# First mixing stage: projections in another order, the inverse between them, attention and units in one loop

## The chip, the cores and the metric

The kernel runs on one core of a Trainium2 chip. The metric is the device time of one execution in microseconds (us); a time is the median of several runs. The engines named here are TensorE (PE in the profile, PEld is its weight load), VectorE (DVE), ScalarE (ACT), GpSimd (POOL) and SyncE (SP), which only issues loads. Each runs its own queue in order, and they meet by semaphores.

## The reference, cut to what matters

Two blocks of two layers each, 512 tokens, width 1024, all in float32. The change lies in the mixer of the second block's first layer. Its input `p = h @ ab_w_in` is split into the columns of differential attention (q, k, v) and those of an RWKV-7 time mix (14 blocks of 128 columns: r, k, v, a low-rank decay and rate input, and a gate input):

```python
p = h @ ab_w_in[j]
qa, ka, va = split_cols(p[..., :A_COLS], A_SIZES)
oa = diff_attention(qa, ka, va, ...)      # 4 heads, softmax(q0 k0) - lam * softmax(q1 k1), times v, rmsnorm
ob = rwkv7_time_mix(p[..., A_COLS:], ...) # 8 heads of 64, state 64x64 per head
mix = jnp.concatenate([oa, ob], axis=-1) @ ab_w_out[j]
x = x + mix
```

Attention, per head and block of 128 queries: two masked softmaxes over up to 512 keys, mixed, times the values. The time mix shifts its input by one token (`mu`), makes from the low-rank input a decay (`w0`, `w2`) and a rate (`a0`, `a2`), normalises the key per head (`kk`), and runs per head `S = S * w + (S @ a) b^T + v k^T`, with `y = S @ r`; then a group norm, a bonus term of `r * rk * k`, and a gate.

## The kernel before, in words

Activations lie transposed: channels on the 128 partitions, the 512 tokens along the free axis. Every f32 product with a weight is three `fp32r` matmuls (high by high, high by low, low by high). A weight chunk (128 x 1024) is loaded by SyncE into one of two raw buffers; ScalarE makes its high part (`weights_hi`, L433), VectorE the low part (`weights_lo`, L445), into a ring of four. Both run three chunks ahead and stand in the queues among the other work: step n makes chunk n + 2. A projection is 24 matmuls of 512 columns. PSUM has eight banks; `K.take` makes TensorE wait until the bank's last user has been read.

The stage (`ab_tensor`, `ab_vector`, `ab_scalar`, `ab_gpsimd`; the order is written out by hand, one list for each engine) runs so:

1. Fourteen rwkv projections in the order `MIXED`: keys (4 to 7), then 12 (decay and rate input) and 13 (gate input), then r and v blocks in turn. VectorE drains each (`ab_project_vector`, times 1/rms), ScalarE scales its own copy, and VectorE adds the shifted one (`mixed_in`). Between them stand the small steps of the time mix for each of four pairs of heads a: `ab_low_tensor` (two low-rank matmuls), `ab_rates_scalar` (two sigmoids and a scaling of the rate for the key), `ab_sums_vector` (a scan of decays), `ab_decays_scalar` (exps), `ab_kk_vector`, `ab_bonus_tensor`, `ab_decayed_vector`, and `ab_lower_tensor`/`ab_lower_vector` (the strictly lower 32 x 32 blocks L, always in banks 6 and 7). Three work tiles (`E.sets`) exist twice, and a uses set a % 2.
2. Four q and four k projections with rope; GpSimd turns rows by DMA (`turn_gpsimd`). The rest of step 1's small steps lies here. When all of L is there, GpSimd takes it through DRAM so that each partition holds one 32 x 32 block (M). Then `linear_tok`: the values, 96 matmuls.
3. `ab_inverse_vector`, the inverse of the triangular blocks on VectorE: part 0 (two 16 x 16 diagonal blocks, rows 14 down to 0), parts 1 to 8 (the off-diagonal block). Parts 0 and 1 stand before attention, parts 2 to 8 between its steps, half a part a step.
4. Attention, 16 steps (head hd, query block t), as a pipeline over 20: scores in banks 0 to 3 (two pairs in turn), mask and maximum on VectorE (L2164, L2167), exp on ScalarE (L2379), mix on VectorE, a transposing matmul with a diagonal (`pt`), values (`pv`).
5. The inverse goes back through DRAM to L. Then 16 units i of the time mix (pair of heads a, 128 tokens t) as a pipeline over 18: `rwkv_b` (four transposes; the ml products in banks 1 and 2, masked by VectorE), `rwkv_c`, `rwkv_d`, `rwkv_e` (G, R and N in banks 4, 6 and 5). The row norm of attention (`rs`, spreads, `y2a`) lies in its first steps.
6. The chain of 15 states (`E.state(n)`), each from the last by a matmul and a VectorE add. Then the output projections and the next layer.

The pieces are tied by order: what a list puts behind a waiting instruction waits as well.

Of the kernel before, what the change touches and what calls it, by code (L numbers as in the profile page):

```python
# [16 lines left out]
P = 128  # L17
# [143 lines left out]
class Kernel:  # L161


    def __init__(self, nc, io, ctx):
# [14 lines left out]
        if self.base > before:  # L179
# [18 lines left out]
                    for i in range(NH)]  # L198
        at += 2 * NH * SLOT
# [1475 lines left out]
NC = 16  # L1675

# [40 lines left out]
class Ab:  # L1717
# [3 lines left out]
    def __init__(self, K):  # L1721
# [29 lines left out]
        sets = [self.vt[:, i, :] for i in range(4)] + [spare[:, 0:T], spare[:, T:2 * T]]  # L1751
        self.sets = [sets[0:3], sets[3:6]]
        self.M = spare[:, 0:1024].rearrange("p (s t) -> p s t", s=32)
        self.blocks = spare.rearrange("p (b z) -> p b z", b=2)[:, :, 0:512].rearrange("p b (j t) -> p b j t", t=32)
        self.tm = raw[:, 0:1024]

        H = K.hmem
        self.sqa = H[:, 0:2048].rearrange("p (k n) -> p k n", k=4)
        self.ya = H[:, 2048:4096].rearrange("p (k n) -> p k n", k=4)
        self.pr = [H[:, 4096 + T * i:4096 + T * i + T] for i in range(6)]  # L1760
        self.pt = [H[:, 7168 + T * i:7168 + T * i + T] for i in range(2)]
        self.dg = [K.nb[0][:, P * i:P * i + P] for i in range(3)]
# [8 lines left out]
                            vt[:, 640 * i:640 * i + 640], nb[:, T * i:T * i + T]) for i in range(3)]  # L1771
# [29 lines left out]
    def scores(self, K, i):  # L1801

        return K.ps[:, 2 * (i % 2):2 * (i % 2) + 2, :]
# [47 lines left out]
def ab_bonus_tensor(K, w, a):  # L1851
    acc = K.take(w, ("bonus", a), K.V)
    w.wait_ge(*K.V["rk", a])
    mm(w.e, v4(acc), K.cc("bones"), K.ab.be(a), True, True).then_inc(*K.P.up(("bonus", a)))
# [14 lines left out]
def ab_attention_tensor(K, w):  # L1869
    E, e = K.ab, w.e  # L1870
    w.wait_ge(*K.V["k", "rope", 3])
    for i in range(20):
        if i < 16:
            hd, t = i // 4, i % 4
            both = E.scores(K, i)
            for c in range(2):
                r = slice(64 * c, 64 * c + 64)
                K.take(w, ("score", i, c), K.A, bank=2 * (i % 2) + c)
                done = mm(e, both[:, c, 0:(t + 1) * P], E.q[r, hd, t * P:(t + 1) * P], E.k[r, hd, 0:(t + 1) * P],
                          True, True)  # L1880
# [1672 lines left out]
```

## Time and profile before

| | |
|---|---|
| median of 3 runs | 2768.85 us (2764.5 to 2778.71) |
| the profiled execution | 2759.99 us |
| its span in the profile | 2758.2 us |
| TensorE busy | 2653.2 us (96%) |
| VectorE busy | 1453.7 us (53%) |
| ScalarE busy | 985.1 us (36%) |
| mean granted TensorE clock | 0.977 |

Times in the profile count from the start of the span. Busy is the time in which an engine works on at least one instruction. The granted clock is the share of full TensorE speed (2.4 GHz) that the chip allowed; 0.50 is 1.2 GHz. An f32 matmul shows as two instructions. In brackets behind an instruction stands how long its engine was idle before it and who ended that. The changed stage lies between 881.8 and 1240.6 us.

### The profile page before, as it was taken

What the parts mean: (1) busy time and instruction counts of PE and PEld (TensorE: products, weight loads), DVE (VectorE), ACT (ScalarE), POOL (GpSimd) and SP (SyncE); (2) the same over time, 40 slices, a digit from 0 to 9 for tenths busy, and PEclk for the clock granted to TensorE, in tenths of its full rate; (3) what the DMA queues carried; (4) which work ended last, traced back from release to release, by engine and by line L of the source; (5) the groups of instructions that cost most, each with busy time, mean ns of one, the idle gap of its engine ahead of it and who ended that gap; (6) DMA issues with size and microseconds to landing.
All of it is one profiled execution on the core that took longest, in us unless ns stands there. A gap on an engine that the chain in (4) does not pass through costs nothing.

```text
span 2758.2 us, 32180 instructions
## 1 busy us (share of the span) xinstructions
PE 2653.2 (96%) x13236; PEld 2112.1 (77%) x13236; DVE 1453.7 (53%) x1905; ACT 985.1 (36%) x1660; POOL 528.3 (19%) x554
## 2 busy tenths in 40 slices
PE   8989998999999998899999999999999998999998
PEld 7777877788888665686788888888878745888886
DVE  8875995643434688546433334343354466533432
ACT  3235545422323533543322223222233445322221
POOL 5711001322200020101222102221002124222200
PEclk9999999999999998899999999999999989999999
DMA  4433112222232231002232332323323300222332
GB/s 154 100 96 113 62 46 69 84 100 93 96 102 93 71 99 32 28 2 69 100 100 92 95 104 92 99 98 93 102 78 122 116 16 1 78 98 99 97 93 86
DMA packets 76932, 232.19 MB, mean 84 GB/s; under 512 B 14961, under 2 KB 16241, under 8 KB 76529
## 3 DMA queue, kind: packets, MB, share of 16 engines
q1 hardware_dynamic: 64176, 212.46, 23.8%
q0 software_dynamic: 4400, 9.71, 1.6%
q10 hardware_dynamic: 8208, 7.96, 0.9%
q8 instruction: 104, 1.70, 0.3%
q14 instruction: 44, 0.35, 0.0%
HBM read 220.13 MB, written 5.77 MB: 82 GB/s over the span
## 4 chain that ended last, share of the span: by engine, by line
PE 78%; DVE 10%; ACT 5%; POOL 4%; issue 1%; DMA 0%; ACTq 0%; DVEq 0%; POOLq 0%
PE ps L358 78%; POOL mem L375 3%; DVE mem L375 3%; DVE part L445 2%; ACT part L433 1%; DVE mem L388 1%; PE ps L369 1%; ACT mem L509 0%; POOL mem L3269 0%; DVE mem L393 0%; DVE mem L3032 0%; DVE mem L408 0%; DVE mem L553 0%; DVE mem L634 0%; DVE mem L2167 0%
## 5 line engine op out<-in xcount | busy, mean ns | idle before, releaser
L358 PE MATMUL ps<-part,part 128*128 128x512 f32 (+1 forms) x9870 | 2249.8, 389 | 33.0 <-DVE part L445 8.5
L358 PEld LDWEIGHTS ps<-part,part 128*128 128x128 f32 x9870 | 1838.7, 189 | 439.6 <-issue 15.8
L445 DVE TENSOR_TENSOR part<-mem,part 128x1024 fp32r<-128x1024 f32 (+2 forms) x419 | 563.2, 1351 | 597.6 <-ACT part L433 597.3
L433 ACT ACTIVATE part<-mem 128x1024 fp32r<-128x1024 f32 (+2 forms) x419 | 415.6, 1003 | 241.9 <-DMA mem<-in_ffa_down 55.9
L375 DVE TENSOR_TENSOR mem<-ps,mem 128x512 f32<-128x512 f32 (+1 forms) x266 | 176.7, 664 | 297.1 <-PE ps L358 288.1
L358 PE MATMUL ps<-mem 128*64 128x64 f32 (+13 forms) x2568 | 264.5, 310 | 35.8 <-ACT mem L2385 10.3
L358 PEld LDWEIGHTS ps<-mem 128*64 128x64 f32 (+5 forms) x2568 | 180.7, 165 | 109.5 <-issue 41.5
L517 POOL TENSOR_TENSOR mem<-mem 128x512 f32<-128x512 f32 x62 | 80.6, 1300 | 713.2 <-ACT mem L509 712.2
L1669 POOL TENSOR_TENSOR mem<-mem 128x512 f32<-128x512 f32 x88 | 113.8, 1293 | 381.5 <-ACT mem L1657 381.5
L1671 POOL TENSOR_TENSOR part<-mem,part 128x512 fp32r<-128x512 f32 x88 | 113.8, 1293 | 353.0 <-ACT part L1660 353.0
L1660 ACT ACTIVATE part<-mem 128x512 fp32r<-128x512 f32 x88 | 55.6, 632 | 327.9 <-DVE mem L375 327.9
L1657 ACT ACTIVATE mem<-mem 128x512 f32<-128x512 f32 x88 | 55.6, 632 | 313.3 <-DVE mem L375 313.2
L522 ACT ACTIVATE part<-mem,prm 128x512 fp32r<-128x512 f32 x56 | 40.4, 722 | 241.1 <-DVE mem L636 169.6
L375 DVE TENSOR_TENSOR mem<-mem 128x512 f32<-128x512 f32 (+15 forms) x205 | 109.6, 534 | 26.5 <-PE ps L358 8.4
L375 POOL TENSOR_TENSOR mem<-mem 128x32 f32<-128x32 f32 (+5 forms) x83 | 85.2, 1026 | 178.6 <-ACT mem L1545 172.0
L636 DVE SCALAR_TENSOR_TENSOR mem<-ps,mem 128x512 f32<-128x512 f32 x32 | 22.1, 692 | 172.6 <-PE ps L358 172.6
L1405 DVE SCALAR_TENSOR_TENSOR mem<-mem,prm 128x512 f32<-128x512 f32 x142 | 97.1, 750 | 0.2
L358 PE MATMUL ps<-mem,cst 128*128 128x512 f32 (+9 forms) x162 | 81.8, 607 | 8.5 <-DVE mem L375 4.1
L3269 POOL TENSOR_TENSOR mem<-mem 128x512 f32<-128x512 f32 (+3 forms) x64 | 45.8, 736 | 123.8 <-DVE mem L375 123.7
L509 ACT ACTIVATE mem<-mem 128x512 f32<-128x512 f32 x64 | 39.6, 618 | 66.7 <-DVE mem L636 66.7
L358 PE MATMUL ps<-cst,mem 128*64 128x64 f32 (+2 forms) x360 | 53.9, 291 | 9.0 <-ACT mem L1145 8.2
L1704 POOL DMA_DIRECT2D mem<-mem x56 | 27.5, 498 | 169.9 <-PE ps L358 107.1
(191 smaller groups left out, 1182.8 us busy)
## 6 DMA issues: line engine op xcount, KB each, us to landing
mem<-in_ffa_gate SPq DMA_DIRECT2D x44, 512.0 KB, 3.3
mem<-in_ffa_up SPq DMA_DIRECT2D x44, 512.0 KB, 3.3
mem<-in_ffb_gate SPq DMA_DIRECT2D x44, 512.0 KB, 3.2
mem<-in_ffb_up SPq DMA_DIRECT2D x44, 512.0 KB, 3.3
mem<-in_ffa_down SPq DMA_DIRECT2D x32, 512.0 KB, 3.5
mem<-in_ffb_down SPq DMA_DIRECT2D x32, 512.0 KB, 3.5
mem<-in_w_odd SPq DMA_DIRECT2D x24, 512.0 KB, 3.3
mem<-in_w_ab SPq DMA_DIRECT2D x22, 512.0 KB, 3.2
```

What stands on the lines that cost most here:

```text
L358: return e.matmul(out, l, r, start=start, stop=stop, skip_group_check=True)
L375: w.e.tensor_tensor(out, a, b, op).then_inc(*w.own.up(*names))
L433: w.e.activation(K.wts[c % NH].h[:, 0:n], K.raws[c % NR][:, 0:n], ACT.Copy).then_inc(*K_A.up(("w", c)))
L445: w.e.tensor_tensor(t.l, K.raws[c % NR][:, 0:n], t.hf, SUB).then_inc(*K.V.up(("w", c)))
L517: w.e.tensor_tensor(ss, ss, sq[k % 2], ADD).then_inc(*K.G.up(("ss", s, k)))
L522: w.e.activation(K.h[k].h, K.x[:, k, :], ACT.Copy, scale=gain(k)).then_inc(*K.A.up(("h", s, k)))
L1405: e.scalar_tensor_tensor(out=c, in0=g[:, k:k + T], scalar=K.pc("conv_w", 31 * o + k), in1=c, op0=MUL, op1=ADD).then_inc(*K.V.up(("tap", o, ...
L1657: w.e.activation(t, t, ACT.Silu).then_inc(*K.A.up(("silu", s, o)))
L1660: w.e.activation(K.hidden.hid[o].h, t, ACT.Copy).then_inc(*K.A.up(("hid", s, o)))
L1669: w.e.tensor_tensor(t, t, K.rstd, MUL).then_inc(*K.G.up(("factor", s, o)))
L1671: w.e.tensor_tensor(K.hidden.hid[o].l, t, K.hidden.hid[o].hf, SUB).then_inc(*K.G.up(("hid", s, o)))
L3269: w.e.tensor_tensor(pr, pr, E.st[u % 4][:, 4 + g:5 + g].to_broadcast([P, n]), MUL).then_inc(*K.G.up(("npr", u, g)))
```

## The change: what it does

- `MIXED` becomes `[12, 4, 5, 6, 7, 0, 8, 1, 9, 2, 10, 3, 11, 13]`: the decay and rate input is projected first, then the keys; the gate input last. The four low-rank pairs follow projections 2 and 3, the sigmoids of all four a stand in ScalarE's steps 3 and 4, the decays in its steps 5 and 6, the head sums of the key norm behind projection 6 (before 5).
- `E.sets` has four sets, taken from the space of q, k and v; `wait`s keep the owners apart. The bonus product goes to `sets[a][2]` and not to `be(a)`.
- L(0) to L(3) follow projections 11, 12, 13 and q(0). L is taken through DRAM after the turn of q(1), M read after that of q(2). The diagonal blocks of the inverse (`ab_diagonal_vector`) stand in six pieces between the q and k projections, parts 1 to 6 before the loop, parts 7 and 8 in its first step.
- Attention and units are one loop of 22 steps; the unit u = j - 4. Scores use banks 1 and 2 only, the pair that the ml products of the units also use; `pt` has bank 6, the head outputs bank 7, G moves into the second half of R's bank 4. Probabilities and `wide` move into three slots of the weight ring.
- The norm of attention's rows comes at the loop's end; two spreads in its last step, two in the chain of states, with `spread` and `y2a` of VectorE between its states.

```diff
-MIXED = [4, 5, 6, 7, 12, 13, 0, 8, 1, 9, 2, 10, 3, 11]
+MIXED = [12, 4, 5, 6, 7, 0, 8, 1, 9, 2, 10, 3, 11, 13]
...
 def ab_tensor(K, w):
...
-        if n == 5:
+        if n == 2 or n == 3:
+            ab_low_tensor(K, w, 2 * n - 4)
+            ab_low_tensor(K, w, 2 * n - 3)
+        if n == 6:
             ab_heads_tensor(K, w, "kk", E.be, lambda a: K.A["kk2", a])
...
+        if n == 8 or n == 9:
+            ab_spread_tensor(K, w, "kk", 2 * n - 16, E.factors)
+            ab_spread_tensor(K, w, "kk", 2 * n - 15, E.factors)
+        if n > 10:
+            ab_lower_tensor(K, w, n - 11)
...
+            if n == 0:
+                ab_lower_tensor(K, w, 3)
+            if 0 < n < 5:
+                ab_bonus_tensor(K, w, n - 1)
...
+def ab_units_tensor(K, w):
+
     w.wait_ge(*K.V["k", "rope", 3])
+    for j in range(STEPS_AB):
+        u = j - DELAY
+        if j < 16:
+            ab_score_tensor(K, w, j)
+        if 0 <= u - 1 < 16:
+            rwkv_c_tensor(K, w, u - 1)
+        if 0 <= u - 2 < 16:
+            rwkv_e_tensor(K, w, u - 2)
+        if 0 <= j - 2 < 16:
+            ab_turned_probs_tensor(K, w, j - 2)
+        if 0 <= u < 16:
+            rwkv_b_tensor(K, w, u)
+        if 0 <= u - 1 < 16:
+            rwkv_d_tensor(K, w, u - 1)
+        if 0 <= j - 3 < 16:
+            ab_values_tensor(K, w, j - 3)
...
 def ab_vector(K, w):
...
-        if n == 6:
+        if n == 4 or n == 5:
+            ab_sums_vector(K, w, 2 * n - 8)
+            ab_sums_vector(K, w, 2 * n - 7)
+        if n == 7:
             rstd_vector(K, w, ("ms", "kk"), E.factors[0:8, :], K.acc("ms", "kk")[0:8, :], 1.0, 1e-12)
...
+        if n == 8:
+            for a in range(4):
+                ab_keys_vector(K, w, a)
+        if 9 <= n < 13:
             ab_kk_vector(K, w, n - 9)
+        if n > 11:
+            ab_lower_vector(K, w, n - 12)
...
+    diagonal = ((14, 9), (8, 6), (5, 5), (4, 3), (2, 2), (1, 1))
...
+        if o > 2:
+            ab_diagonal_vector(K, w, *diagonal[o - 3])
...
+def ab_units_vector(K, w):
+
+    E = K.ab
+    for j in range(STEPS_AB):
+        u = j - DELAY
+        if j < 16:
+            ab_max_vector(K, w, j)
+        if 0 <= j - 1 < 16:
+            ab_mix_vector(K, w, j - 1)
+        if j == 0:
+            ab_inverse_vector(K, w, 7)
+            ab_inverse_vector(K, w, 8)
+        if 0 <= u - 2 < 16:
+            rwkv_e_vector(K, w, u - 2)
...
+        if 0 <= u < 16:
+            rwkv_ml_vector(K, w, u)
+        if 0 <= u + 1 < 16:
+            rwkv_b_vector(K, w, u + 1)
...
 def ab_scalar(K, w):
...
+        if n == 2:
+            w.wait_ge(*K.V["mixed_in", 0])
+            e.activation(E.wa[0:64, :], E.wa[0:64, :], ACT.Tanh).then_inc(*K.A.up("wa"))
+        if 3 <= n < 7:
+            a = n - 3
+            w.wait_ge(*K.V["mixed_in", 1 + a])
             e.activation(E.al(a), E.ka(a), ACT.Copy, scale=K.pc("kk", a)).then_inc(*K.A.up())
             w.wait_ge(*K.A.now)
             e.activation(E.be(a), E.al(a), ACT.Square).then_inc(*K.A.up(("kk2", a)))
-        if n == 4:
+        if n == 3 or n == 4:
+            ab_rates_scalar(K, w, 2 * n - 6)
+            ab_rates_scalar(K, w, 2 * n - 5)
+        if n == 5:
             w.wait_ge(*K.V["lam"])
             e.activation(E.lam[:, 2:4], E.lam[:, 0:2], ACT.Exp).then_inc(*K.A.up("lam"))
+        if n == 5 or n == 6:
+            ab_decays_scalar(K, w, 2 * n - 10)
+            ab_decays_scalar(K, w, 2 * n - 9)
+        if n == 7:
+            for a in range(4):
+                ab_keys_scalar(K, w, a)
             rstd_scalar(K, w, ("ms", "kk"), E.factors[0:8, :])
```

## Rows read from the trace of the kernel before

**Rows 1.** The page: chain that ended last, shares by engine.
```profile
PE 78%; DVE 10%; ACT 5%; POOL 4%; issue 1%; DMA 0%; ACTq 0%; DVEq 0%; POOLq 0%
```
**Rows 2.** Windows: stretch, its us; PE, PEld, DVE, ACT, POOL busy; granted clock; DMA.
```profile
881.80:976.90 95.10, 89.03 (x350) 62.71 (x349) 61.73 (x78) 47.76 (x65) 0.00 (x0) 0.98 0.23 76
976.90:1058.80 81.90, 77.59 (x356) 61.43 (x356) 66.38 (x108) 24.05 (x34) 19.46 (x37) 0.94 0.34 97
1058.80:1120.60 61.80, 44.53 (x232) 29.54 (x232) 49.58 (x96) 35.20 (x109) 3.71 (x5) 0.83 0.06 18
1120.60:1222.25 101.65, 93.91 (x1163) 77.61 (x1163) 52.06 (x93) 55.90 (x153) 10.55 (x16) 0.92 0.03 9
1222.25:1240.57 18.32, 16.36 (x465) 14.70 (x465) 6.61 (x16) 0.37 (x1) 0.00 (x0) 1.00 0.01 3
```
**Rows 3.** Timeline of TensorE: start, us, line, shape, count [idle before].
```profile
881.82 27.49 PE L358 MATMUL ps<-part,part 128*128 128x512 f32 x120
...
965.48 1.13 PE L358 MATMUL ps<-mem 64*128 64x512 f32 x4
...
994.56 2.08 PE L358 MATMUL ps<-mem 64*128 64x128 f32 x16 [3.52 <-DVE mem L375]
...
1017.06 1.16 PE L358 MATMUL ps<-mem 64*128 64x128 f32 x16
...
1036.84 22.06 PE L358 MATMUL ps<-part,part 128*128 128x512 f32 x96 [0.75 <-ACT mem L1687]
```
**Rows 4.** Timeline of ScalarE: a copy, a table load, a sigmoid, decays, weight copy.
```profile
894.98 0.72 ACT L2443 ACTIVATE mem<-mem 128x512 f32<-128x512 f32 x1 [2.09 <-DVE mem L375]
...
933.37 1.28 ACT L2400 ACT_TABLE_LOAD   x1
934.66 0.69 ACT L2400 ACTIVATE mem<-ps,prm 128x512 f32<-128x512 f32 x1
...
948.57 0.63 ACT L2414 ACTIVATE mem<-mem 128x512 f32<-128x512 f32 x1
...
950.55 1.04 ACT L433 ACTIVATE part<-mem 128x1024 fp32r<-128x1024 f32 x1
```
**Rows 5.** Timeline of VectorE: low part, mix, products, L, inverse part 0, ml mask.
```profile
951.63 1.23 DVE L445 TENSOR_TENSOR part<-mem,part 128x1024 fp32r<-128x1024 f32 x1
...
953.68 0.75 DVE L388 SCALAR_TENSOR_TENSOR mem<-mem,prm 128x512 f32<-128x512 f32 x1
...
960.20 3.60 DVE L375 TENSOR_TENSOR mem<-mem 128x512 f32<-128x512 f32 x5
...
992.72 1.78 DVE L375 TENSOR_TENSOR mem<-ps,cst 32x256 f32<-32x256 f32 x4
...
1044.54 0.09 DVE L403 MEMSET mem<- 128x32 f32 x1 [1.57 <-DMA mem<-scratch]
...
1056.81 0.62 DVE L408 TENSOR_REDUCE mem<-mem 128x30 f32<-128x450 f32 x1
...
1170.79 0.96 DVE L375 TENSOR_TENSOR mem<-ps,cst 128x768 f32<-128x768 f32 x1 [1.00 <-PE ps L358]
```
**Rows 6.** Windows of five us, columns as rows 2: two with low clock.
```profile
995.00:1000.00 5.00, 5.00 (x22) 3.45 (x21) 3.73 (x6) 1.07 (x2) 0.00 (x0) 0.50 0.34 104
...
1135.00:1140.00 5.00, 5.00 (x18) 2.77 (x18) 0.96 (x1) 2.12 (x6) 0.00 (x0) 0.50 0.00 0
```
**Rows 7.** Window of ten units, columns as rows 2.
```profile
1164.20:1215.10 50.90, 50.90 (x722) 44.77 (x721) 25.52 (x51) 31.62 (x91) 5.56 (x9) 1.00 0.01 2
```
**Rows 8.** Groups of VectorE from 1061.5 to 1120.6: busy, mean ns, idle before.
```profile
L2167 DVE TENSOR_REDUCE mem<-ps 128x2 f32<-128x256 f32 (+3 forms) x16 | 13.2, 825 | 0.6
...
L375 DVE TENSOR_TENSOR mem<-mem 128x768 f32<-128x768 f32 (+3 forms) x7 | 8.2, 1170 | 0.2
L2164 DVE TENSOR_TENSOR ps<-ps,cst 128x256 f32<-128x256 f32 x15 | 6.4, 426 | 2.9 <-PE ps L358 2.8
L408 DVE TENSOR_REDUCE mem<-mem 128x64 f32<-128x768 f32 (+3 forms) x7 | 5.3, 763 | 0.2
```

More of the change, by code:

```diff
@@ L198, in __init__ @@
                     for i in range(NH)]
+        self.slots = [mem[:, at + 2 * i * SLOT:at + 2 * (i + 1) * SLOT] for i in range(NH)]
         at += 2 * NH * SLOT
@@ new lines, in ab_score_tensor, with ab_turned_probs_tensor @@
+def ab_score_tensor(K, w, i):
+    E = K.ab
+    hd, t = i // 4, i % 4
+    both = E.scores(K)
+    for c in range(2):
+        r = slice(64 * c, 64 * c + 64)
+        K.take(w, ("score", i, c), K.A, bank=1 + c)
+        done = mm(w.e, both[:, c, 0:(t + 1) * P], E.q[r, hd, t * P:(t + 1) * P], E.k[r, hd, 0:(t + 1) * P], True, True)
+    done.then_inc(*K.P.up(("score", i)))
+def ab_turned_probs_tensor(K, w, u):
+    E = K.ab
+    acc = K.take(w, ("pt", u), K.A, bank=6)
+    w.wait_ge(*K.V["mixed_pr", u])
+    w.wait_ge(*K.A["diag", u])
+    for kt in range(u % 4 + 1):
+        done = mm(w.e, acc[:, kt * P:(kt + 1) * P], E.pr[2 * u % 6][:, kt * P:(kt + 1) * P], E.dg[u % 3], True, True)
+    done.then_inc(*K.P.up(("pt", u)))
@@ L2120, in ab_lower_vector, with ab_diagonal_vector, ab_inverse_vector @@
     K.V.also(("L", a), ("L", a, 0), ("L", a, 1))
-def ab_inverse_vector(K, w, part, steps=(0, 1)):
+def ab_diagonal_vector(K, w, first, last):
+    E = K.ab
+    B, tm = E.blocks, E.tm
+    if first == 14:
+        w.wait_ge(*K.counts["shuffle"]["M"])
+        memset(w, E.M.rearrange("p s t -> p (s t)")[:, 0:1024:33], 1.0)
+    for s in range(first, last - 1, -1):
+        n = 15 - s
+        tmv = tm[:, 0:2 * n * n].rearrange("p (b t j) -> p b t j", b=2, t=n)
+        tt(w, tmv, B[:, :, s + 1:16, s + 1:16].rearrange("p b j t -> p b t j"),
+           b(B[:, :, s, s + 1:16], [P, 2, n, n], 2), MUL)
+        reduce(w, B[:, :, s, s + 1:16], tmv, ADD)
+def ab_inverse_vector(K, w, part):
     E = K.ab
@@ new lines, in ab_inverse_vector, with ab_max_vector @@
+        tt(w, tmv, b(B[:, 0, s0:s0 + 4, s0:16], [P, 4, 16, n], 2),
+           b(M12[:, s0:16, :].rearrange("p j t -> p t j"), [P, 4, 16, n], 1), MUL)
+        reduce(w, M12[:, s0:s0 + 4, :], tmv, ADD, *(["inverse"] if part == 8 else []))
+def ab_max_vector(K, w, i):
+    E = K.ab
+    t = i % 4
+    n = (t + 1) * P
+    both, st = E.scores(K), E.st[i % 4]
+    w.wait_ge(*K.P["score", i])
+    w.e.tensor_tensor(both[:, :, t * P:n], both[:, :, t * P:n], b(K.cc("negmask"), [P, 2, P], 1), ADD).then_inc(
+        *K.V.up())
+    w.wait_ge(*K.V.now)
+    w.e.tensor_reduce(st[:, 0:2], both[:, :, 0:n], AX, MAX, negate=True).then_inc(*K.V.up(("max", i)))
@@ L2394, in ab_rates_scalar @@
 def ab_rates_scalar(K, w, a):
     E = K.ab
-    if a > 1:
-        w.wait_ge(*K.V["decayed", a - 2])
     w.wait_ge(*K.P["decay", a])
-    w.e.activation(E.sets[a % 2][0], K.acc("decay", a), ACT.Sigmoid, bias=K.pc("w0", a)).then_inc(
+    w.e.activation(E.sets[a][0], K.acc("decay", a), ACT.Sigmoid, bias=K.pc("w0", a)).then_inc(
         *K.A.up(("decay", a)))
```

505 lines of the change are left out of this document (225 added, 280 removed).

## The prediction

> **What bounds the kernel now.** I read the chain that ended last first: TensorE holds 78% of it and VectorE 10% [rows 1], so a step counts only where it makes TensorE wait or lets it stop waiting. The change lies in one stage, so I next read that stage in five stretches [rows 2]: the rwkv projections 1 to 13 (95.1 us), q, k and av (81.9), attention (61.8), the units (101.65) and the chain of states (18.3). The reader is to see where TensorE is idle: 6.1 us of the first, 4.3 of the second, 17.3 of the third and 7.7 of the fourth. In the third VectorE is busy 49.6 of 61.8: it bounds attention, because the inverse sits between its steps. In the middle of the fourth TensorE has no gap at all and a unit costs 50.9/10 = 5.09 us [rows 7]. So 17 + 8 us of gaps can be won by laying attention over the units. To win them the change starts its VectorE work earlier and reorders the first two stretches; I then ran each engine's queue through them, with the durations of rows 3 to 5, from 881.8 us, where TensorE starts projection 1.
>
> **Stretch 1, projections 1 to 13 (before 95.1).** TensorE's work: 13 projections at 27.49/5 = 5.50 [rows 3] are 71.5; four pairs of low-rank matmuls at 1.13, 4.5; four head sums and four spreads, each one matmul of 512 columns, priced at 1.0 by that same row, 8.0; three L blocks at 1.1, 3.2. Sum 87.2. To it come these waits:
> - After projection 2 (ends 892.8) the low-rank pair needs tanh. ScalarE ends the projection's own copy at 895.7 [rows 4], loads a table (1.28), takes the tanh (0.6, as the sigmoid): 897.6. Wait 4.8.
> - After projection 3 the second rate matmul needs the bank of decay(0), and the next ones those of the following sigmoids. They come behind, on ScalarE: VectorE's drain 0.7, own copy, key copy and square 0.65 each, table load 1.28, four sigmoids at 0.6: 6.5 us after the projection's end. TensorE has 1.4 of work for it. Wait 5.1. Projection 4 starts at 912.0.
> - After projection 6 (ends 928.4) the last head sum needs the square of key 3. From the end of projection 5 (922.9, rates done at about 922.5) run: weight copy 1.0, its low part 1.25, drain 0.7, own copy, key copy and square 1.95, table load 1.5 with the small exp, two sets of decays at 1.98 (948.57 to 950.55 [rows 4]) 4.0, weight copy 1.0, low part 1.25, drain 0.7, and the last three ScalarE steps 1.95: 938.1. TensorE has three head sums (about 2.9) meanwhile. Wait 6.8. It is the queue that counts: projection 6's drain on VectorE stands behind a low part whose high part stands behind the decays.
> - After projection 8, four key scalings (2.9) on ScalarE and the reciprocal on VectorE: wait 1.0.
> - L(1) takes the banks of L(0), which VectorE empties at the end of its step 12: drain 0.7, mix 0.75, four operations of kk(3) at 0.72 [rows 5], L(0) 1.78, with gaps 6.3. L(2) likewise: 0.7 + 0.75 + 1.78 and gaps, 3.4.
> Waits 27.4, against 6.1 before. 87.2 + 27.4 = 114.6: **+19.5**.
>
> **The clock.** After the wait of 3.52 us at 994.56 [rows 3] the granted clock was 0.50 over the next 5 us [rows 6], the lower of the two levels; that and the rest of the recovery cost about 3 us. Four of the new waits are longer than that one; 4 x 3 = 12 at most on the path, and some of it is absorbed by the wait behind it. I take **+9**; ends 0 and 20.
>
> A table switch is in three of these waits. The row shows a load of 1.28 us and the sigmoid starting at 934.66, right behind it [rows 4]. The Trainium skill (ScalarE: Activation LUTs, What ACT_TABLE_LOAD costs) gives about 1.38 us of drain beside each load. By it the three waits would be longer by 4.1 us together and the forecast 2783; the rows show no drain, so the measurement decides.
>
> **Stretch 2, q, k, av (before 83.9 to VectorE's first score at 1060.8).** VectorE's queue from the start of q(0): eleven low parts 13.0, eight ropes at 2.1, 16.8, L(2) and L(3) 3.6, bonus products and outputs 5.8, decayed products (8) 5.8, mix, cos and sin 3.6, the diagonal blocks of the inverse 12.9 (1044.54 to 1057.43 [rows 5]), its part 1 3.3 and parts 2 to 6 10.8 (seven pieces 8.2 + 5.3 [rows 8] less parts 7 and 8, 2.8). Sum 75.6. Waits for turned rows and the first transfer of M about 5, and it starts 1 us early: 79.7, **-4.2**. TensorE's own work there is 44 + 1.1 + 3.7 + 22.1 [rows 3] = 71: the moved inverse is not hidden to its end; TensorE stands about 8 us before the loop, on VectorE.
>
> **Stretch 3, the loop (before 161.4 from 1060.8 to the first state).** Work of TensorE: 16 units at 5.09 are 81.4; attention 44.5 busy at a granted 0.83 [rows 2], some 39 at full clock with its four norm sums; two row spreads 2.1: 122. A step has 5.09 + 35/16 = 7.3 of TensorE. VectorE has 4.8 us a step (25.5/10 of units [rows 7] and (49.6 - 13.5)/16 of attention) and ScalarE 5.4 (31.6/10 and 35.2/16), so both fit. Gaps: scores have one pair of banks now, so in steps 0 to 3 score (0.8), mask and maximum (19.6/16 [rows 8]) and exps (1.1) follow one another, 3.4 a step and 1.2 for parts 7 and 8: 15 in all, of which TensorE works 5: +10. Steps 4 and 5 +2.6, steps 6 to 15 0.3 each (the ml masks, 0.96 [rows 5], before the next score, with only 0.7 to 1.5 of TensorE work between), tail 1.5. Sum 139. The clock: 1135 to 1140 was busy throughout and still at 0.50 [rows 6]; the loop starts after an 8 us wait and five light steps, +8. 147: **-14.4**; ends 130 and 165.
>
> **Stretch 4, the states (before 18.3).** Two spreads on TensorE (+1.1); the eight VectorE pieces of 0.7 fit into the idle of 18.3/15 - 6.6/15 = 0.78 of each state [rows 2]: **+1.1**, at worst +4.
>
> **Sum.** 19.5 + 9 - 4.2 - 14.4 + 1.1 = +11.0 us. The profiled execution, 2759.99, would become 2771; it is 8.9 below the median of the three runs, 2768.85, so the predicted median is 2780. A measurement of this kernel can tell some 0.5% (13.8 us) from no change: 2755 to 2783 is the same.
>
> **Rivals.** (a) The loop packs as meant: 8 us of fill on 122 give 130, and the clock in stretch 1 costs 2 because TensorE still issues small matmuls in the waits. 19.5 + 2 - 4.2 - 31.4 + 1.1 = -13, near 2755, and with 3 us less waiting there 2752: faster. For it: TensorE had no gap in ten units. Against it: the waits of stretch 1 follow from queue order. (b) Slower: the single pair of banks. Score, maximum, exp (3.4 together, as above), ml matmuls (0.9, estimated), ml mask, next score is a ring through three engines; on average 5.3 us, and with the longest tiles, whose maximum and exps take half as long again, about 7, near TensorE's own 7.3. It decides from a step of 7.6 on; at 8.8 it adds 1.2 x 16 = 19: 2799. (c) The clock stays at its lower level behind each wait longer than in the one row: 20 in place of 9, and 2791: slower. (d) The change does not do what it says: ScalarE or VectorE in the loop hold the units back to where they were, 161 for the loop: 2794, slower; it shares its chance with (b).
>
> **Chances.** Forecast 0.44, (a) 0.16, (b) with (d) 0.26, (c) 0.14. Faster 0.16, same 0.44, slower 0.40. The likeliest case alone reaches from 2764 to 2790; the range 2752 to 2802 leaves out the outer part of (a) and of (b).
>
> **What would show it.** The first q projection starts some 28 us later than the 976.9 of before, with TensorE waits of 4 to 7 us after projections 2, 3, 6 and 12 ended by ScalarE or VectorE; the granted clock is lower behind them; TensorE waits about 8 us before the first score; then a step of the loop takes 7.3 to 7.9 us with TensorE busy nearly throughout; and the first state comes near 1232. It is wrong if the waits in the projections are under 15 us together, if the loop takes under 135 or over 160, or if the states take over 23.

## The result, and the profile after

| | before | after |
|---|---|---|
| median | 2768.73 us (8 runs, 2764.43 to 2778.71) | 2788.82 us (8 runs, 2780.72 to 2795.85) |
| ratio | | 1.0067, 95% interval 1.0052 to 1.0082 |
| profiled execution | 2759.99 us | 2787.78 us |
| the stage, first rwkv projection after its entry to the first output matmul | 881.82 to 1240.57, 358.75 us | 892.77 to 1266.71, 373.94 us |
| mean granted TensorE clock | 0.977 | 0.970 |

The change makes the kernel slower by 0.67%, 18.6 us by the ratio. The stage in the profile is 15.2 us longer; it is entered 10.95 us later and what lies behind it takes 1.7 us more. Those two parts run unchanged code. How far they move by themselves is an experiment below; so from here on the stage alone is compared.

The chain that ended last, on the page after: TensorE and VectorE hold a little more of it [rows 1].

```profile
PE 80%; DVE 11%; ACT 5%; issue 1%; POOL 1%; DMA 0%; ACTq 0%; DVEq 0%; POOLq 0%
```

The windows of the kernel after that answer to the stretches of before [rows 2, 7]: projections to q(0), then q, k and values, then the wait and the loop, four steps and more of the loop alone, and the states. Columns as there.

```profile
892.77:1019.15 126.38, 100.09 (x394) 71.56 (x393) 71.26 (x94) 50.82 (x73) 0.00 (x0) 0.88 0.18 57
1019.15:1091.50 72.35, 71.60 (x310) 57.14 (x309) 59.02 (x94) 16.18 (x20) 19.52 (x37) 0.97 0.38 110
1091.50:1242.05 150.55, 129.54 (x1395) 103.11 (x1393) 94.02 (x181) 88.20 (x262) 13.62 (x21) 0.91 0.05 15
1141.70:1215.20 73.50, 70.59 (x853) 59.56 (x852) 43.71 (x94) 47.41 (x150) 6.57 (x11) 1.00 0.01 2
1242.05:1266.71 24.66, 23.10 (x470) 20.84 (x469) 12.38 (x24) 2.52 (x4) 0.00 (x0) 0.73 0.01 2
```

The reader is to see 26.3 us of TensorE idle in the first (6.1 before), and a clock of 0.88 where it was 0.98; almost no gap in the second; a loop whose middle runs at full clock; and a chain of states at 0.73 where it ran at 1.00.

The waits of the first stretch, in the timeline of TensorE after (start, duration, line, shape, count, idle before and its releaser):

```profile
908.73 3.78 PE L359 MATMUL ps<-mem 64*128 64x512 f32 x8 [4.79 <-ACT mem L2592]
...
923.82 3.23 PE L359 MATMUL ps<-mem 64*128 64x512 f32 x6 [3.76 <-ACT mem L2540]
926.97 17.00 PE L359 MATMUL ps<-part,part 128*128 128x512 f32 x72
...
953.74 1.88 PE L359 MATMUL ps<-mem,cst 128*8 128x512 f32 x2 [7.09 <-ACT mem L2598]
...
1004.46 2.08 PE L359 MATMUL ps<-mem 64*128 64x128 f32 x16 [6.38 <-DVE mem L376]
1006.47 7.28 PE L359 MATMUL ps<-part,part 128*128 128x512 f32 x24
...
1017.14 2.08 PE L359 MATMUL ps<-mem 64*128 64x128 f32 x16 [3.39 <-DVE mem L376]
```

They are tanh (4.79), the rate's bank (3.76, after 1.1 of work), the square of key 3 (7.09), the banks of L(0) (6.38) and of L(1) (3.39); 0.88 lies between. The clock shows in the durations: a projection of 24 matmuls takes 7.28 right behind a wait, and 17.00/3 = 5.67 once it has recovered; two L blocks' 16 matmuls take 2.08 in place of 1.16.

The entry of the loop, same view:

```profile
1092.62 0.49 PE L359 MATMUL ps<-mem 64*128 64x128 f32 x4
1103.79 1.57 PE L359 MATMUL ps<-mem 64*128 64x256 f32 x4 [10.67 <-ACT mem L2440]
1107.82 2.82 PE L359 MATMUL ps<-mem 64*128 64x384 f32 x6 [2.47 <-ACT mem L2440]
1112.14 4.21 PE L359 MATMUL ps<-mem 64*128 64x512 f32 x10 [1.50 <-ACT mem L2440]
```

TensorE has issued the first score and stands 10.67 us for VectorE's first maximum and the exps behind it; each further score waits for the ring of mask, maximum and exp.

The chain of states, same view, and two windows inside it:

```profile
1240.08 2.03 PE L359 MATMUL ps<-mem,cst 4*128 4x512 f32 x4 [1.00 <-ACT mem L559]
1242.05 6.92 PE L359 MATMUL ps<-mem 64*64 64x64 f32 x128
1248.90 1.12 PE L359 MATMUL ps<-mem,cst 4*128 4x512 f32 x2
1249.95 1.12 PE L359 MATMUL ps<-mem 64*64 64x64 f32 x32
1251.00 1.12 PE L359 MATMUL ps<-mem,cst 4*128 4x512 f32 x2
1252.05 9.16 PE L359 MATMUL ps<-mem 64*64 64x64 f32 x192
...
1266.71 3.02 PE L359 MATMUL ps<-part,part 128*128 128x512 f32 x12 [0.90 <-DVE mem L376]
```

```profile
1243.00:1248.00 5.00, 5.00 (x100) 5.00 (x98) 2.77 (x5) 1.26 (x2) 0.00 (x0) 0.50 0.00 0
...
1252.00:1257.00 5.00, 5.00 (x95) 4.95 (x96) 2.75 (x5) 1.26 (x2) 0.00 (x0) 0.51 0.02 3
```

TensorE is busy in every one of these ten microseconds and yet at the lower level of 1.2 GHz. In windows of one microsecond the clock is at 0.50 from 1242 to 1248.7 and again from 1252 to 1258.5, 13 of the 24.7 us. A state is 16 matmuls, 32 records; the 128 at 1242.05 are four states in 6.92, 1.73 each, against the 18.3/15 = 1.22 of before.

### The profile page after: what moved, and what is told of

It reads as the page before. It is cut to its first block, busy times and chain, and to the rows that moved or that the text cites. A ratio compares the mean times of both kernels' runs of the same rounds, so it can differ in the third digit from the quotient of the medians.

```text
span 2786.0 us, 32135 instructions
## 1 busy us (share of the span) xinstructions
PE 2663.1 (96%) x13236; PEld 2126.6 (76%) x13236; DVE 1461.0 (52%) x1905; ACT 978.7 (35%) x1659; POOL 524.6 (19%) x554
## 4 chain that ended last, share of the span: by engine, by line
PE 80%; DVE 11%; ACT 5%; issue 1%; POOL 1%; DMA 0%; ACTq 0%; DVEq 0%; POOLq 0%
PE ps L359 80%; DVE mem L376 4%; DVE part L446 2%; ACT part L434 1%; PE ps L370 1%; DVE part L376 1%; ACT mem L510 0%; DVE mem L409 0%; DVE mem L3145 0%; POOL mem L3382 0%; DVE mem L389 0%; DVE mem L394 0%; DVE mem L554 0%; DVE mem L635 0%; ACT mem L3335 0%
## 5 line engine op out<-in xcount | busy, mean ns | idle before, releaser
L359 PE MATMUL ps<-mem 128*64 128x64 f32 (+11 forms) x2568 | 261.9, 312 | 47.6 <-ACT mem L2440 16.1
L376 DVE TENSOR_TENSOR mem<-mem 128x512 f32<-128x512 f32 (+14 forms) x205 | 113.8, 555 | 19.4 <-ACT mem L1187 7.8
```

Source lines behind the costliest of these rows:

```text
L359: return e.matmul(out, l, r, start=start, stop=stop, skip_group_check=True)
L376: w.e.tensor_tensor(out, a, b, op).then_inc(*w.own.up(*names))
```

## The experiments

All are written against the kernel after; where a section says that a kernel builds on spread_low or one_load, its edit is shown against that one. Where a median stands, it comes with the ratio to the kernel before on the same chip. The stage is the stretch defined above, in the profiled execution of each. For every kernel that was timed, the stage less the 358.75 us of before agrees within 5 us with what its ratio says of 2770 us.

| | stage us | median us | ratio (95%) |
|---|---|---|---|
| after | 373.9 | 2788.82 | 1.0067 (1.0052 to 1.0082) |
| split | 408.7 | 2819.18 | 1.0164 (1.0138 to 1.0191) |
| early_l | 359.5 | 2775.63 | 1.0006 (0.9989 to 1.0023) |
| late_decays | 367.4 | 2782.17 | 1.0026 (1.0009 to 1.0043) |
| spread_low | 346.9 | 2761.68 | 0.9950 (0.9930 to 0.9971) |
| pool_low | 349.4 | 2766.38 | 0.9969 (0.9953 to 0.9986) |
| delay5 | 350.4 | 2768.39 | 0.9981 (0.9957 to 1.0006) |
| late_inverse | 355.9 | 2767.93 | 0.9979 (0.9963 to 0.9996) |
| norm_split | 343.8 | 2757.70 | 0.9958 (0.9938 to 0.9977) |
| before_again | 358.2 | one run, 2770.23 | |
| one_load | 346.9 | one run, 2759.68 | |
| norm_late | 349.3 | one run, 2764.68 | |
| rows_after | 376.5 | one run, 2790.16 | |

### before_again: how far unchanged code moves

The kernel before, once more, no edit.

> The kernel before, profiled once more, to see how far the part ahead of the stage, which the change does not touch, moves from one execution to the next. If the 10.95 us by which the changed kernel's profile entered the stage later (892.77 against 881.82) is variation between executions, this profile enters between 882 and 893, with a total that is higher by about as much, and the stage itself again takes 358 to 360 us. If the changed kernel's code costs something ahead of the stage, it enters at 882 to 883 again.

Measured: it enters at 882.01, which by itself decides nothing, and the stage takes 358.2. But this execution took 10.2 us longer than the first, and all of it lies behind the stage (span 2768.4 against 2758.2, first output matmul at 1240.19 against 1240.57). The kernels of this study, all with the same code ahead of the stage, entered it between 880.73 (norm_split) and 893.61 (early_l). So some 10 us of either unchanged part is variation between executions, and neither the 10.95 ahead of the stage nor a single total says anything of the change. The guess that a fixed cost sits ahead of it fell with norm_split and late_inverse (881.12).

### split: what laying attention over the units is worth

```diff
-DELAY = 4
+DELAY = 19
...
-        if j > 20:
-            for hd in (2 * j - 42, 2 * j - 41):
+        if j == 21:
+            for hd in (0, 1):
...
-        if j >= 7 and j % 4 == 3:
+        if 7 <= j < 20 and j % 4 == 3:
```

(beside the delay, this keeps the number of row spreads and of copies of attention's outputs as it was)

> The changed kernel with a lag of 19 steps in place of 4, so that attention runs alone and the units follow it; everything else stays, the inverse between the projections too. Theory (the loop wins by laying attention over the units): the stretch from VectorE's first score to the first state, 139.7 us in the changed kernel, grows to attention alone at the score ring's 3.9 us a step (62) and units at 5.09 with their start (98), 158 to 162; the time is 18 to 22 us above the changed kernel, near 2809. Rival (the loop's saving came from taking the inverse out of attention, and the overlap gives nothing more, since score, maximum and exp hold the units back): the stretch stays under 146 and the time within 6 us of the changed kernel, 2783 to 2795.

Measured: 2819.18, 27 us above the kernel after by the ratios (0.0097 x 2773). Its stage is 34.7 longer. From VectorE's first score to the first state pass 177.6 us, against 139.7 in the kernel after and an expected 158 to 162: the theory holds, and the size was put too low. The 27 us are what the overlap is worth within this order; against the kernel before, which ran attention and units apart in 161.4 us with two pairs of score banks, the loop gains 21.7. TensorE's timeline of split:

```profile
1128.26 2.33 PE L359 MATMUL ps<-mem 64*128 64x512 f32 x8 [0.91 <-ACT mem L2440]
1134.46 9.64 PE L359 MATMUL ps<-mem 128*128 128x128 f32 x48 [3.88 <-ACT mem L2468]
...
1203.82 2.83 PE L359 MATMUL ps<-mem 128*128 128x64 f32 x52 [0.47 <-DVE mem L376]
```

Alone, the score steps wait 3.9 us a head for the head's copies (L2468), and each unit 0.47 for VectorE; in the merged loop other work fills both. The loop is a gain; the loss is elsewhere.

### early_l: the banks of L

VectorE reads L(0) to L(2) one projection earlier, directly behind the matmuls that made them.

```diff
-        if n > 11:
-            ab_lower_vector(K, w, n - 12)
+        if n > 10:
+            ab_lower_vector(K, w, n - 11)
...
         if o == 0:
-            ab_lower_vector(K, w, 2)
```

> The changed kernel, with only VectorE's reading of the blocks L(0), L(1), L(2) one projection earlier (behind projections 11, 12, 13). Theory (the six waits of TensorE in the projections are the loss, and each is the order of one queue): the waits of 6.38 and 3.39 us behind projections 12 and 13 go, and with them the low clock behind them, 10 to 15 us less than the changed kernel, near 2776. Rival (the waits are hidden in VectorE's lateness at the loop's entry, which is then 10 us more of waiting there): the time stays within 3 us of the changed kernel.

Measured: 2775.63, ratio 1.0006: this edit alone takes back 14.4 us of the stage and brings the changed kernel level with the one before. TensorE's timeline of early_l, at L(2):

```profile
1006.41 1.16 PE L359 MATMUL ps<-mem 64*128 64x128 f32 x16 [0.65 <-DVE mem L376]
```

The wait of 6.38 at L(1) is gone and that of 3.39 at L(2) has become 0.65, 9.1 us in all, and a block's matmuls take 1.16 in place of 2.08: the waits took the clock with them, which is the other 5 us. At TensorE's first score early_l is 14.4 us ahead of the kernel after. Behind it the loop takes 1.7 us more and the states 2.3 less, with the same code in both.

### late_decays: ScalarE's queue ahead of the last square

```diff
-        if n == 5 or n == 6:
-            ab_decays_scalar(K, w, 2 * n - 10)
-            ab_decays_scalar(K, w, 2 * n - 9)
+        if n == 6:
+            ab_decays_scalar(K, w, 0)
+            ab_decays_scalar(K, w, 1)
...
             rstd_scalar(K, w, ("ms", "kk"), E.factors[0:8, :])
+            ab_decays_scalar(K, w, 2)
+            ab_decays_scalar(K, w, 3)
```

> The changed kernel, with only ScalarE's decays (0, 1) behind the square of key 3 in step 6 and decays (2, 3) behind the norm factor in step 7, before in steps 5 and 6 ahead of that square. Theory: TensorE's wait of 7.09 us for the last head sum falls to under 2, with the clock 6 to 9 us less than the changed kernel, near 2781. Rival (TensorE then waits as long for the spreads or for weights, as ScalarE's work is only shifted): within 3 us of the changed kernel, 2786 to 2792.

Measured: 2782.17, stage 6.5 us shorter than after. TensorE's timeline of late_decays, at the last head sum and at L(1):

```profile
949.64 1.02 PE L359 MATMUL ps<-mem,cst 128*8 128x512 f32 x2 [3.31 <-ACT mem L2598]
...
999.08 2.08 PE L359 MATMUL ps<-mem 64*128 64x128 f32 x16 [7.36 <-DVE mem L376]
```

7.09 fell to 3.31, not to the "under 2" of the theory, and 1.0 of it came back at L(1), 6.38 to 7.36. The median came within 1.2 us of the 2781 expected.

### spread_low: the low-rank pairs apart, with both edits above

```diff
-        if n == 2 or n == 3:
-            ab_low_tensor(K, w, 2 * n - 4)
-            ab_low_tensor(K, w, 2 * n - 3)
+        if n == 3 or n == 5:
+            ab_low_tensor(K, w, n - 3)
+            ab_low_tensor(K, w, n - 2)
```

(and the sigmoids in ScalarE's steps 3 and 5, the sums in VectorE's steps 4 and 6)

> The changed kernel with both edits above and the low-rank pairs taken apart: pairs 0, 1 behind projection 3 and pairs 2, 3 behind projection 5, their sigmoids in ScalarE's steps 3 and 5, their sums in VectorE's steps 4 and 6. Theory: all six waits in the projections (27.4 us) fall to under 5 and the granted clock in that stretch rises from 0.88 to 0.97 or more; the stretch goes from 126.4 to 92 to 97 us. Some 25 to 32 us less than the changed kernel, 2757 to 2764, which is below the kernel before by 5 to 12. Rival (VectorE, not TensorE, bounds from projection 9 to the loop, so the waits move to the loop's entry): 10 to 15 less than the changed kernel, with a TensorE wait of over 20 us before the second score.

Measured: 2761.68, ratio 0.995 (0.9930 to 0.9971): faster than both kernels. Its projections take 99.5 us to q(0) where the kernel after takes 126.4. The time came as expected (2757 to 2764), the stretch did not quite: its waits are 8.8 us together and not under 5, its clock is 0.95 and not 0.97, and 92 to 97 us had been put. TensorE's timeline of spread_low at three of the waits left:

```profile
933.95 1.88 PE L359 MATMUL ps<-mem,cst 128*8 128x512 f32 x2 [5.36 <-ACT mem L2597]
...
979.54 1.16 PE L359 MATMUL ps<-mem 64*128 64x128 f32 x16 [1.85 <-DVE mem L376]
...
1070.89 1.57 PE L359 MATMUL ps<-mem 64*128 64x256 f32 x4 [10.72 <-ACT mem L2439]
```

Its stage is 27.0 us shorter than that of the kernel after, with the same loop: the order of small steps in the projections was the loss, and the loop doesn't need it.

### one_load: a wait that only moves

```diff
-        if n == 5:
-            w.wait_ge(*K.V["lam"])
-            e.activation(E.lam[:, 2:4], E.lam[:, 0:2], ACT.Exp).then_inc(*K.A.up("lam"))
...
         if n == 6:
+            w.wait_ge(*K.V["lam"])
+            e.activation(E.lam[:, 2:4], E.lam[:, 0:2], ACT.Exp).then_inc(*K.A.up("lam"))
             ab_decays_scalar(K, w, 0)
```

> spread_low, with ScalarE's small exp of lambda behind the square of key 3 and directly ahead of the decays, which use the same table. Theory (ScalarE's queue sets the 5.36 us wait before the last head sum): one table load (1.28) and the small exp leave the queue ahead of the square, the wait falls to 3.9 to 4.1 us and the q projections start 1.3 us earlier. Rival (VectorE's drain and mix of projection 6 come last there, whatever ScalarE does): the wait stays within 0.4 us of 5.36.

Measured: the wait fell as the theory says, and the rest did not. TensorE's timeline of one_load:

```profile
928.97 1.88 PE L359 MATMUL ps<-mem,cst 128*8 128x512 f32 x2 [3.84 <-ACT mem L2597]
...
975.22 2.08 PE L359 MATMUL ps<-mem 64*128 64x128 f32 x16 [2.89 <-DVE mem L376]
```

5.36 became 3.84, but L(1)'s wait grew by 1.0 (1.85 to 2.89) with a lower clock behind it (2.08 for the block in place of 1.16), and a new one of 0.28 came where the 0.67 at L(2) went; q(0) starts 99.3 us after the entry (99.5 in spread_low), and the stage is 346.9 in both. From projection 8 on it is VectorE's queue, 5.6 us a step and 7.6 with an L block, that sets the pace.

### pool_low: GpSimd in VectorE's place

The low parts of the four value chunks on GpSimd, otherwise spread_low.

```diff
-            out.append((io[name][k:k + 2].rearrange("k p n -> p k n"), 2 * n, False))
+            out.append((io[name][k:k + 2].rearrange("k p n -> p k n"), 2 * n, name == "w_av"))
...
+        if n > 5:
+            weights_lo_gpsimd(K, w, K.first[4] + 17 + n)
...
+    weights_lo_gpsimd(K, w, K.first[4] + 26)
```

> spread_low, with the low parts of the four value chunks made by GpSimd, which stands idle there, and not by VectorE. Theory: TensorE's wait of 10.72 us before the second score is VectorE's queue of the second stretch (inverse, ropes, low parts: 81.3 us against 71.5 of TensorE). Four low parts of 1.22 leave it: the wait falls by 4.5 to 5 us to about 6, and the median by as much, near 2757 where spread_low had 2762. Rival: GpSimd takes longer over them (its 128x256 operation took 0.67 us, so 128x1024 about 2.7, and more if the two engines slow each other), so the values' matmuls wait for their chunks, or VectorE's own operations grow by what was saved: the first score comes less than 2 us earlier and the time is the same or up to 5 us more.

Measured: the rival. The wait before the second score grew from 10.72 to 15.31 and the stage by 2.5 us. The median is 2766.38, 4.7 above spread_low's, but the two intervals of the ratio overlap. VectorE's timeline of pool_low, and then GpSimd's over the same time:

```profile
1033.77 5.07 DVE L376 TENSOR_TENSOR mem<-mem 128x512 f32<-128x512 f32 x4
...
1039.31 5.58 DVE L376 TENSOR_TENSOR mem<-mem 128x288 f32<-128x288 f32 x1
```

```profile
1033.77 2.42 POOL L458 TENSOR_TENSOR part<-mem,part 128x1024 fp32r<-128x1024 f32 x1
...
1039.66 4.75 POOL L458 TENSOR_TENSOR part<-mem,part 128x1024 fp32r<-128x1024 f32 x2
```

The same product of 128x288 on VectorE in spread_low:

```profile
1038.37 0.70 DVE L376 TENSOR_TENSOR mem<-mem 128x288 f32<-128x288 f32 x1
```

0.70 became 5.58: VectorE's operation began just before GpSimd's two of 2.4 us and ended when both were over. Three such places cost 2.3, 4.9 and 2.1 us, 9.3 in all, against 4.9 saved. The Trainium skill (Trainium Architecture — The Big Picture, What this means for kernel authors) calls the port that the two share an exclusive lock and not a split of bandwidth; by that rule, the trace agrees: the 0.35 us ahead of GpSimd's two and the 0.48 behind them are enough for the whole of VectorE's 0.70, so nothing of it need have gone on beside them.

### delay5 and late_inverse: the loop's entry

Both build on spread_low.

```diff
-DELAY = 4
+DELAY = 5
```

(and the two spreads of the loop stay in its step 21, as in split) and for late_inverse also

```diff
-    for part in range(1, 7):
+    for part in range(1, 5):
...
-        if j == 0:
-            ab_inverse_vector(K, w, 7)
-            ab_inverse_vector(K, w, 8)
+        if j < 2:
+            ab_inverse_vector(K, w, 5 + j)
+        if j == 2:
+            ab_inverse_vector(K, w, 7)
+            ab_inverse_vector(K, w, 8)
```

> spread_low, with the units five steps behind attention, not four. It is the control for late_inverse. TensorE has one more light score step before the first unit (about 3.5 us of ring for 2.2 of its work, so +1.3) and one more step of units alone at the end, in which the norm's reciprocals and root lie a step further from the chain of states, so the waits of 1.0 us at the loop's end go. Sum near zero: within 2 us of spread_low's stage (346.9 us). If the fall of the clock at the start of the chain stands on those waits, it goes too and the stage is 2 to 4 us shorter.

> delay5, with parts 5 and 6 of the inverse in the loop's first two steps and parts 7 and 8 in its third. Theory (the wait of 10.7 us at the loop's entry is VectorE's queue): the first score comes 5.6 us earlier, the parts fill VectorE's idle 1.9 and 2.1 of the steps behind, and the inverse is back through DRAM (9.2 us) about when unit 0 wants it. The entry wait falls to about 5, the stage is 2 to 4 us shorter than delay5's. Rival: the score ring of VectorE and ScalarE pays for each part in full, and unit 0 waits for the transfer: the stage stays within 1 us of delay5's, since it is then the inverse's end plus its transfer, not the first score, that starts the units.

Measured: delay5's stage is 3.5 us longer than spread_low's, outside the 2 us expected, late_inverse's 5.5 longer again. In late_inverse the entry wait fell from 11.19 to 7.62, but the three that follow grew (2.79, 2.02, 1.56), a later one of 1.58 became 2.77, and the clock, back at 1.00 for a few us in between, was at 0.50 again from 1083 to 1103, where delay5 stayed at 1.00 from 1088 on. VectorE waits 2.25 for the inverse's transfer before the first unit: the units start when the inverse is back, and earlier scores bought nothing, as the rival said; the size of the loss was foreseen by neither. In delay5 the units alone at the loop's end bring a wait of their own for the ml mask, queued on VectorE behind 3.52 us of reciprocals. TensorE's timeline of delay5:

```profile
1202.74 5.46 PE L359 MATMUL ps<-mem 128*128 128x64 f32 x60 [2.86 <-DVE mem L376]
```

Over ten runs each, the two differ by nothing (0.9981 and 0.9979), so the 5.5 us between their profiles is not shown by their times.

### rows_after, norm_late, norm_split: what lowers the clock in the states

rows_after moves all four spreads of the kernel after behind the chain. norm_late (on spread_low) cuts the norm's reciprocals in four between states 3 to 6 and issues the spreads at states 9, 10, 12 and 13. norm_split (on one_load):

```diff
-        if c == 4 or c == 5:
-            ab_rows_tensor(K, w, c - 2)
+        if c in (4, 5, 8, 9):
+            w.wait_ge(*K.A["rstd", ("ms", "subln")])
+            ab_rows_tensor(K, w, (4, 5, 8, 9).index(c))
...
             recip(w, E.rs[0:4, 0:256], E.rs[0:4, 0:256])
+        if j == 21:
             recip(w, E.rs[0:4, 256:T], E.rs[0:4, 256:T], ("inverse", ("ms", "subln")))
```

(not shown: the loop has no spread any more, the square root stands behind the loop on ScalarE, and VectorE's steps for the spreads stand behind states 6, 7, 10 and 11)

> The changed kernel, with all four row spreads and what VectorE does with them behind the chain of states. Theory: the granted clock falls in the states because of what the spreads bring (two four-matmul spreads with their waits at 1240.08 and 1248.90 to 1252, each followed by 0.50). Then the chain of states runs at 1.00 and takes 18.3 to 19 us, as in the kernel before; behind it TensorE issues 2.1 us of spreads and waits about 3 for VectorE and ScalarE (0.75 + 0.6 + 0.7 for the first row block, 1.45 for each further one against 0.7 of matmuls), and from the first state to the first output matmul pass 23 to 24 us against 24.66. Rival: it is the thinned end of the merged loop, or the small matmuls of the states, that brings the clock down; then the chain shows 0.50 for 5 us or more again, takes 21 to 23, and 26 to 28 us pass.

> spread_low, with the reciprocals of attention's row norm (3.5 us of VectorE in one piece, ahead of the last unit's steps in the queue) cut into four and put between the additions of states 3 to 6, the square root behind the last unit's copies on ScalarE, and the row spreads at states 9, 10, 12 and 13. From the last unit's group of matmuls (the one with the wait of 0.56) to the first output matmul passed 21.1 us in the kernel before, 29.9 in the changed one and 32.4 with all spreads behind the chain, where the clock fell to 0.50 at the chain's start behind a wait of 1.90, with no spread before it. Theory: the first fall of the clock comes from TensorE's waits at the loop's end, which stand behind the reciprocals; then the chain starts at 1.00 behind waits of 0.57 and 0.56, and 25 to 27 us pass (21.1, 2.1 of spreads, up to 3 for a second fall behind the spreads). Rival: the clock falls there whatever the norm does, because the last steps of the loop are light; then the chain's start is at 0.50 again and 28 us or more pass.

> one_load, with the second half of the reciprocals of attention's row norm (1.76 us of 3.5) behind VectorE's last unit step, the square root behind ScalarE's copies of the last unit, and the row spreads at states 4, 5, 8 and 9. In norm_late the chain began at a clock of 1.00 behind waits of 0.56 and 0.58, but its states came 1.50 us apart while the reciprocals lay between them, and a fall of the clock followed in its second half. Theory (waits of TensorE around the loop's end bring the falls): the waits stay at about 0.6, no reciprocal lies between the states, the chain runs at 1.00 but for a few us, and from the last unit's group with the wait of 0.56 to the first output matmul pass 24 to 27 us against 29.9 of spread_low. The stage takes 341 to 344 us against 346.9, and the median comes near 2758 where spread_low had 2762 (ratio 0.993 to 0.994). Rival: the four spreads of 512 columns from four rows, or a period of their own, bring the falls, so two falls of 5 us come again; 28 to 30 us pass and the ratio is 0.995 as for spread_low.

Measured, from the last unit's group with its wait of 0.56 to the first output matmul: before 21.1 us, after 29.9, rows_after 32.4, norm_late 31.9, norm_split 30.6. TensorE's timeline of rows_after, and two windows of it:

```profile
1233.29 19.49 PE L359 MATMUL ps<-mem 64*64 64x64 f32 x464 [1.90 <-ACT mem L2490]
1252.71 5.74 PE L359 MATMUL ps<-mem,cst 4*128 4x512 f32 x8
1261.57 4.53 PE L359 MATMUL ps<-part,part 128*128 128x512 f32 x12 [3.12 <-DVE mem L376]
```

```profile
1237.00:1240.00 3.00, 3.00 (x62) 3.00 (x62) 0.85 (x2) 0.00 (x0) 0.00 (x0) 0.50 0.03 5
...
1246.00:1249.00 3.00, 2.74 (x80) 2.52 (x82) 0.88 (x3) 0.00 (x0) 0.00 (x0) 1.00 0.00 0
```

Here the clock falls at the chain's start with no spread before it, behind a wait of 1.90, and 28.3 us pass from the first state to the first output matmul where 23 to 24 were expected: that first fall does not need the spreads, so the theory does not hold as put. With that wait cut to about 0.6, in norm_late and norm_split, the chain starts at 1.00: the first fall comes with TensorE's waits at the loop's end (from the one of 1.00 on in these runs), where the last unit's copies stand behind the norm's reciprocals and root. But a second fall then came behind the spreads, and a long one: 17 us in norm_late, 14 in norm_split. TensorE's timeline of norm_split and a window:

```profile
1196.81 1.12 PE L359 MATMUL ps<-mem 64*64 64x64 f32 x32 [0.58 <-ACT mem L2489]
1198.44 3.54 PE L359 MATMUL ps<-mem 64*64 64x64 f32 x96 [0.51 <-DVE mem L376]
1201.91 1.12 PE L359 MATMUL ps<-mem,cst 4*128 4x512 f32 x2
```

```profile
1213.00:1216.00 3.00, 3.00 (x22) 1.43 (x22) 1.16 (x2) 0.63 (x1) 0.00 (x0) 0.50 0.00 0
```

It lasted from about 1205 to 1219. In the kernel after, rows_after, norm_late and norm_split a fall begins 2 to 4 us behind the first spread in or behind the chain, and so it does in late_decays, spread_low, one_load and pool_low. That made the spreads look like the cause of the second fall. Four other kernels speak against it: split, delay5, late_inverse and early_l carry two spreads in the chain too, and the clock stays at 1.00 behind them. early_l has the code of the kernel after here, line for line. It has the first fall (1229 to 1236) and not the second. TensorE's timeline of early_l, and then of delay5:

```profile
1228.09 2.72 PE L359 MATMUL ps<-mem,cst 4*128 4x512 f32 x4 [1.00 <-ACT mem L559]
1230.74 6.29 PE L359 MATMUL ps<-mem 64*64 64x64 f32 x128
...
1239.07 1.12 PE L359 MATMUL ps<-mem,cst 4*128 4x512 f32 x2
1240.12 2.33 PE L359 MATMUL ps<-mem 64*64 64x64 f32 x64
```

```profile
1221.44 1.12 PE L359 MATMUL ps<-mem,cst 4*128 4x512 f32 x2
1222.49 2.33 PE L359 MATMUL ps<-mem 64*64 64x64 f32 x64
```

Two states take 2.33 behind the spreads there, against 9.16/3 = 3.05 behind 1252.05 in the kernel after. From the first state to the first output matmul the same code took 24.7 us in the kernel after and 22.4 in early_l; delay5 and split, at 1.00 throughout, took 21.0. So the spreads alone do not bring the second fall, what does stays open, and part of it differs between executions of equal code. norm_split's gain in stage over one_load (3.0 us) is not at this place (its wait at the loop's entry was 9.52 where one_load had 10.89), and its ratio of 0.9958 is spread_low's 0.995 again. That its stage and its median lie where the theory had put them is luck: the place it changed took 30.6 us and not 24 to 27.

## Why the prediction was right or wrong

The forecast was 2780 with a range from 2752 to 2802; the median is 2788.82, 8.8 above, and the direction, +15.2 us in the stage against a sum of +11.0, was right. The likeliest case was "within 0.5%", at 0.44, and the result lies beyond it, at 0.67%, in what had 0.40. The mechanism was right in its main part: waits that follow from the queues' order in the projections cost more than the loop wins. Of its three signs of being wrong one came: the states took 24.7 us, over 23. Term by term, from profile to profile:

| | forecast us | measured us |
|---|---|---|
| stretch 1, waits and work | +19.5 | +18.4 |
| its clock | +9 | +12.9 |
| stretch 2 | -4.2 | -0.7 |
| loop | -14.4 | -21.7 |
| states | +1.1 | +6.3 |

- **Stretch 1.** The waits were forecast at 4.8, 5.1, 6.8, 1.0, 6.3 and 3.4; they came as 4.79, 3.76, 7.09, 0.88, 6.38 and 3.39, each ended by the engine named. Going through the queues by hand from single durations was exact to 0.3 us in five of six. The other, for the bank of decay(0), was 1.3 too long: 6.5 us of queue had been put behind projection 3, and the bank was free 4.9 behind it. early_l and late_decays show them to be what they were said to be. With the forecast's 87.2 of work and 26.3 idle, 12.9 of the 126.4 are left, which is the clock. The 9 was too little. Four longer waits came and one like the 3.52 of before; at 3 us for each of the four the prediction had 12 "at most" and took off 3 for what a later wait would absorb, and the runs show no such saving. The prediction's side sum with a slower table load comes to 2784 and not 2783; the loads for tanh and the sigmoids took 1.28 us here too, and the function began 0.02 behind each.
- **Stretch 2.** VectorE's waits were priced too low and its work too high. It waited 4.5 for weight parts, 3.2 for turned rows and 3.0 for M, 10.7 where 5 had been put; the rest of the 83.2 us is 72.5, where 75.6 had been put, and the early start of 1 us did not come. The 8 us before the loop became 10.7.
- **The loop.** 147 was forecast, 139 as work and gaps and 8 for the clock; measured are 139.7. The clock was at 0.50 to about 1120, as forecast, but in those steps TensorE waits for the score ring whether it is fast or slow. Adding clock and gaps in full was the error. In the 139.7 us TensorE was idle for 11.8, where 17 had been put, and its 127.9 of busy time leave 5.9 over the 122 of work, where 8 had been put for the clock. A slower TensorE fills part of a gap, so the two lie over one another; no run separates them. Four steps took 29.6 us, 7.4 a step, as forecast (7.3 to 7.6), with 0.83 of wait in every fourth step for a ScalarE copy queued behind the head's two copies.
- **The states.** This step failed. "+1.1, at worst +4" priced only the instructions, and those too low: the loop's sum has 2.1 for two spreads, this one 1.1, and with the clock at 1.00 the same chain takes 21.0 us in split and delay5, 2.7 over the 18.3 of before. The other 3.6 are the chain at 0.50 for 13 of its 24.7 us, at 1.7 a state in place of 1.2. It had no bound for a lower clock because TensorE has no long wait there.
- **Rivals.** (a), faster, did not come: the waits of stretch 1 were real. The ring of (b) with the single pair of banks never set the pace after step 5. (c), more for the clock, is in part what happened, 12.9 and the states in place of 9. (d) did not come: the loop took 139.7 us and not 161, and split, the same order without the overlap, 177.6.
- The sum's errors of +3.9, +3.5 and +5.2 against -1.1 and -7.3 nearly cancel, so the total was closer than its parts, and that is luck: up to the first state they leave 1.0 us, and the prediction's time for it, 350 us behind the entry, was met with 349.3. What is left of the stage's 4.2 is the states. The other 4.6 of the 8.8 are not in the stage.

## What to carry to other kernels

A loop that fills gaps can win what it promises and the kernel still lose, when the small steps moved ahead of it stand in front of something that TensorE needs at once: here a bank read one step late (9 us of waits, 14 with the clock) and exps ahead of a square. After a reordering, list for each engine what its queue now puts ahead of each result that TensorE waits for, and move the reader of a bank right behind its writer. Work through queues instruction by instruction gave five of six waits to a few tenths and the sixth to 1.3 us; the clock behind them has to be priced by rows of as many and as long waits as the change makes.

## What the runs showed of the hardware that was not expected

- A granted clock of 0.50 for six to fourteen us while TensorE was busy the whole time, with 64x64 products and with matmuls of four rows, behind waits of 1.0 to 1.9 us or none; and with equal code twice in one kernel's states (after) and once in another's (early_l).
- A VectorE product of 0.70 us lasted 5.58 while GpSimd ran two operations of 2.4: moving VectorE work to an idle GpSimd cost twice what it saved.
- The same code ahead of and behind the stage differed by 10 us between executions of equal kernels; differences below 0.4% are read from the stage in the profile or from many runs, not from one total.
